# The squares of a norm's second half: four tiles added on GpSimd and summed once on TensorE

## The chip, the core and the metric

The kernel runs on one core of a Trainium2 chip. The metric is the device time of one launch in microseconds. TensorE multiplies matrices, VectorE and ScalarE do elementwise work, GpSimd does slower elementwise work on SBUF, SyncE issues most of the loads. The engines have a queue each and meet at semaphores.

## The reference

Two transformer blocks follow each other on x (1 x 512 tokens x 1024 channels, fp32). Cut to what matters here:

```python
def rms_norm(x, g):
    y = xf * lax.rsqrt(jnp.mean(xf * xf, axis=-1, keepdims=True) + NORM_EPS)
    return (y * g.astype(jnp.float32)).astype(x.dtype)

# first block, after attention and convolution
x = x + (g_a * y_attn + g_b * y_conv) @ w_out[l]
x = x + conv_ffn(rms_norm(x, norm2_g[l]), ffn_w_up[l], ...)
# second block, after its mixing
x = x + gate_m * mixed            # mixed = ... @ w_out[l]
h = rms_norm_2(x, ffn_norm_g[l]) * (1 + scale_f) + shift_f
u, v = jnp.split(h @ w_up[l], 2, axis=-1)
```

The change touches two norms: `norm2_g` of the first block and `ffn_norm_g` of the second. Each stands between the output projection (`w_out`) and the projection up (`w_up`).

## The kernel before

Activations lie turned: channels on the 128 partitions, eight tiles of channels (`KD` = 8), and the 512 tokens in the free dimension. A projection is a run of tiles s, numbered through the whole program; each makes 128 output channels. The first norm stands after tiles `S_OUT` = 50 to 57 and before `S_UP` = 58; the other after `S_OUT2` = 148 to 155 and before `S_UP2` = 156.

**Weights.** Products are split in two parts for precision. For a tile, SyncE loads the raw weights (two tiles a buffer, two buffers), ScalarE rounds them to `w_hi` (`hi`), GpSimd subtracts to get `w_lo` (`lo`, line 778), and TensorE makes three products for each of the eight tiles of its input: `split_product`, lines 2120 to 2122. `hi` waits for its buffers; `lo(s)` waits for `hi_done` and counts `lo_done`, on which both TensorE and the next load into the raw buffer wait.

**The norm in halves.** `split_norm` (VectorE), `split_norm_act` (ScalarE) and `into_split_norm`, `first_sum`, `second_sum` and `ffn_pe` (TensorE) split the tokens in two halves, `COLS[0]` and `COLS[1]`, of 256 each. Index b is 0 for the first norm and 2 for the other. The last four of the eight output tiles are computed half by half. ScalarE squares x in twelve steps q (`square_of`): q 0 to 3 are tiles 0 to 3 in full width, q 4 to 7 the first halves of tiles 4 to 7, q 8 to 11 their second halves, written to `hn` (two buffers) and `sq` (two buffers). VectorE adds the squares q 1 to 7 to `rstd` (`half_add`, semaphore `half_added`). So `rstd` holds in its first half the squares of all eight tiles, in its second half only those of tiles 0 to 3.

The sum over the partitions is a matmul with a 128x128 matrix of ones in plain fp32. `first_sum` (line 2173) makes it once over the first half of `rstd`. `second_sum` makes five into the same PSUM columns: one of `rstd` (line 2177), and one of each of the four squares q 8 to 11 (line 2180), each after a wait for its square. Then ScalarE takes the root (`half_root`, line 879), VectorE the reciprocal (line 1354) and scales the eight tiles of this half (lines 1361, 1369, 1371), ScalarE rounds them.

**The order around the second sum** is written by hand, in each engine's queue:
- TensorE (`ffn_pe`): first halves of the first two up tiles, then `second_sum`, first halves of the third and fourth, then the second halves of all four.
- ScalarE: `hi` of the four up tiles, with the squares 8 to 11 and the rounded pieces of the first half between them; the last `hi` stands just before the last square.
- GpSimd: nothing but the `lo` of the four up tiles (`lo(s)` in loops over s, in the second norm at the end of `hgrn_pool`), then a hardware loop over the rest of the up tiles.
- SyncE: the load for the seventh and eighth up tile waits for the `lo` of the fourth.

Of the kernel before, what the change touches and what calls it, by code (L numbers as in the profile page):

```python
# [10 lines left out]
ALU = mybir.AluOpType  # L11
# [7 lines left out]
KD = D // P  # L19
# [23 lines left out]
S_ATTN, S_CONV, S_OUT, S_UP, S_DOWN = 34, 42, 50, 58, 102  # L43
S_FH, S_QH, S_KV2, S_PAIRED, S_GH = 126, 130, 134, 136, 144
S_OUT2, S_UP2, S_DOWN2, S_END = 148, 156, 200, 224
# [113 lines left out]
def build(nc, a, out):  # L159
# [5 lines left out]
    with ctx:  # L165
# [29 lines left out]
        ones = sb("ones", [P, P])  # L195
        small = sb("small", [P, NSM, P])
        sm = small[:, :, :].rearrange("p a b -> p (a b)")
        rstd = sb("rstd", [P, T])
# [104 lines left out]
        ps = [nc.alloc_psum_tensor(f"ps{i}", [P, 512], F32) for i in range(8)]  # L303
# [14 lines left out]
        squared, summed, rooted, inverted = sem("squared"), sem("summed"), sem("rooted"), sem("inverted")  # L318
        normed, n_hi = sem("normed"), sem("n_hi")
        half_done, x_half, half_added, half_lo = sem("half_done"), sem("x_half"), sem("half_added"), sem("half_lo")  # L320
# [76 lines left out]
        for n in range(S_END // 2):  # L397
            s = 2 * n
# [69 lines left out]
        COLS = [slice(0, HALF), slice(HALF, T)]  # L468
        SPLIT_FROM = [S_OUT, S_FH - 4, S_OUT2]
        SQUARES, SQUARES2, PIECES = 12, KD + 2, 2 * KD  # L470

        SQ_BASE, HALF_SQ = {2: SQUARES, 5: SQUARES2 + 2 * SQUARES}, [0, SQUARES, SQUARES2 + SQUARES]
        HALF_SUM = [0, None, 2]
        HALF_HN = [0, PIECES, 2 * PIECES]
        HALF_ROOT = [QT, QT + 2, QT + 4]
        HALF_DONE, HALF_ADDED = [0, 4, 6], [0, None, KD - 1]


        SUM_COLS = [slice(64 + 4 * half, 68 + 4 * half) for half in range(2)]
# [18 lines left out]
        def square_of(q):  # L498

            k = q if q < KD else q - 4  # L500
            cols = slice(0, T) if q < 4 else COLS[q // KD]
            return k, cols, rstd[:, :] if q == 0 else (hn, sq)[k // 2 % 2][:, k % 2, cols]
# [107 lines left out]
        def hgrn_pool(pool, lo):  # L610

            def level(n):
                b = ALL[n]
                g, f, k = pairs_of(hg, b), pairs_of(hf, b), pairs_of(hk, b)
                if n:
                    kk = pairs_of(keys_at[n], b)
                    earlier = [m for m in range(1, n) if keys_at[m] is keys_at[n]]
                    if earlier:
                        pool.wait_ge(chunk_done, level_done(earlier[-1] + 1))
                    pool.tensor_tensor(kk[:, :, 0, :], k[:, :, 0, :], g[:, :, 0, :], ALU.mult).then_inc(k_scaled, 1)  # L620
                if n < len(ALL) - 1:
                    if n:
                        pool.wait_ge(f_merged, n)
                    pool.tensor_tensor(g[:, :, 0, :], g[:, :, 0, :],
                                       f[:, :, 1, b - 1:b].to_broadcast([P, HG * T // (2 * b), b]),
                                       ALU.mult).then_inc(g_merged, 1)
                    pool.wait_ge(g_merged, n + 1)

            def gated_head(hd):
                pool.wait_ge(r_sq, hd + 1)  # L630
                pool.wait_ge(freed["act"], FREED[S_GH + hd][1])
                pool.tensor_tensor(hq[:, hd, :], hq[:, hd, :], hgo[:, hd, :], ALU.mult).then_inc(r_gated, 1)

            pool.wait_ge(f_ready, 2 * HG)
            level(0)
            lo(S_KV2)
            lo(S_KV2 + 1)
            lo(S_PAIRED)
            lo(S_PAIRED + 1)
            level(1)  # L640
            for s in range(S_PAIRED + 2, S_PAIRED + 5):
                lo(s)
            level(2)
            lo(S_PAIRED + 5)
            level(3)
            level(4)
            lo(S_PAIRED + 6)
            level(5)
            lo(S_PAIRED + 7)
            level(6)  # L650
            lo(S_GH)
            level(7)
            level(8)
            lo(S_GH + 1)
            for s in range(S_GH + 2, S_OUT2 + 1):
                lo(s)
            gated_head(0)
            lo(S_OUT2 + 1)
            for hd in range(1, HG):
                gated_head(hd)  # L660
                if hd == 2:
                    lo(S_OUT2 + hd)
            for s in range(S_OUT2 + 3, S_UP2 + 4):
                lo(s)

        block = ctx.enter_context(nc.Block())

# [87 lines left out]
        @block.gpsimd  # L755
        def _(pool):
            chain = [0]

            def link(ins):
                chain[0] += 1  # L760
                ins.then_inc(pool_chain, 1)
                pool.wait_ge(pool_chain, chain[0])

            link(pool.memset(ident[:, :], 0.0))
            link(pool.affine_select(out=ident[:, :], in_=ident[:, :], compare_op=ALU.not_equal, fill=1.0,
                                    base=0, pattern=[[-1, P]], channel_multiplier=1))
            pool.memset(eps_t[:, :], EPS)
            pool.memset(ones[:, :], 1.0).then_inc(consts, 1)
            link(pool.memset(rows[:, NSM - 1, :], 0.0))
            small_dmas(pool, 1)  # L770

            def lo(s, slot=None, count=None):

                pool.wait_ge(hi_done, s + 1 if count is None else count)
                slot = s if slot is None else slot
                nk = 8 if count is not None else DEPTH_OF[s]
                part = raw[slot // 2 % 2][:, 0:nk * 256].rearrange("p (k n) -> p k n", k=nk)
                pool.tensor_tensor(w_lo[slot % 4][:, 0:nk, :], part[:, :, slot % 2 * P:(slot % 2 + 1) * P],  # L778
                                   w_hi[slot % 4][:, 0:nk, :].bitcast(F32), ALU.subtract).then_inc(lo_done, 1)

            def tables():
                link(pool.iota(dist[:, :], [[-1, T]], base=T - P, channel_multiplier=1,
                               allow_small_or_imprecise_dtypes=True))
                link(pool.affine_select(out=dist[:, :], in_=dist[:, :], compare_op=ALU.is_ge, fill=MASKED,
                                        base=T - P, pattern=[[-1, T]], channel_multiplier=1))
                cpat = [[P, QT], [-CMP_STRIDE, 32]]
                link(pool.iota(cdist[:, :, :], cpat, base=1 - CMP_BLOCK, channel_multiplier=1,
                               allow_small_or_imprecise_dtypes=True))
                link(pool.affine_select(out=cdist[:, :, :], in_=cdist[:, :, :], compare_op=ALU.is_ge, fill=MASKED,
                                        base=1 - CMP_BLOCK, pattern=cpat, channel_multiplier=1))  # L790
                link(pool.memset(cvalid[:, :, :], 1.0))
                pool.affine_select(out=cvalid[:, :, :], in_=cvalid[:, :, :], compare_op=ALU.is_ge, fill=0.0,
                                   base=1 - CMP_BLOCK, pattern=cpat, channel_multiplier=1).then_inc(consts, 1)
                pool.memset(vcN[:, :], 0.0)
                pool.memset(pcT[:, :, :], 0.0)
                pool.memset(z[:, :, 0:PAD], 0.0).then_inc(consts, 1)

            for s in range(S_UP + 4):
                lo(s)
                if s == 2:  # L800
                    tables()
            with pool.Fori(0, FT // 2 - 1) as i:
                for j in range(4):
                    lo(None, S_UP + j, i * 4 + (S_UP + j + 5))
            for s in range(S_DOWN, S_KV2):
                lo(s)
                if S_DOWN + 5 <= s < S_DOWN + 19 and (s - S_DOWN) % 2:
                    masks2(pool, link, (s - S_DOWN - 5) // 2)
                if s in (S_QH, S_QH + 1):
                    for m in range(2):  # L810
                        tables2(pool, link, 2 * (s - S_QH) + m)
            tables2(pool, link, 4)
            hgrn_pool(pool, lo)
            with pool.Fori(0, FT // 2 - 1) as i:
                for j in range(4):
                    lo(None, S_UP2 + j, i * 4 + (S_UP2 + j + 5))
            for s in range(S_DOWN2, S_END):
                lo(s)
# [1298 lines left out]
        def _(pe):  # L2117
# [56 lines left out]

            def second_sum(b):
                pe.wait_ge(normed, HALF_HN[b] + KD)
                pe.matmul(ps[7][:, COLS[1]], ones[:, :], rstd[:, COLS[1]], start=True, stop=False)
                for q in range(KD, SQUARES):
                    pe.wait_ge(squared, HALF_SQ[b] + q + 1)
                    ins = pe.matmul(ps[7][:, COLS[1]], ones[:, :], square_of(q)[2], start=False, stop=q == SQUARES - 1)  # L2180
                ins.then_inc(summed, 1)

            def into_split_norm(b, x, xl, ready, after=lambda n: None):

# [164 lines left out]
            for j in range(1, NI + 2):  # L2349
# [5 lines left out]
                if j <= NI:  # L2355
                    m = j - 1
                    i, t, b = ITEMS1[m]
# [398 lines left out]
```

## Time and profile before

| | us |
|---|---|
| median of 3 runs | 1392.86 |
| the runs | 1390.56 to 1392.98 |
| the profiled execution | 1392.87 |
| its span | 1391.0 |
| TensorE matmul busy | 1377.5 |
| GpSimd busy | 594.9 |
| VectorE busy | 775.9 |
| ScalarE busy | 598.9 |

The span is the stretch from the first to the last instruction in the trace. Busy times are sums over one engine's instructions; matmuls are pipelined, so their records overlap, and the distance between the starts of two of them tells what one costs. In the rows PE is TensorE, DVE VectorE, ACT ScalarE, POOL GpSimd and SP SyncE; names stand as out<-in. `few` in a row is the small tile of epsilons.

### The profile page before, as it was taken

Reading aid. Unit: us, or ns where it says so; the run is one execution under the profiler, and the core shown is the slowest. Engines: PE = TensorE matmul, PEld = TensorE weight load, DVE = VectorE, ACT = ScalarE, POOL = GpSimd, SP = SyncE. Lnnn points to the kernel's source line nnn. Section 1 sums busy time; section 2 is a strip of 40 time slices with the busy share of each in tenths; the row PEclk is TensorE's granted clock in tenths of the full one; section 3 lists DMA queues with packets and bytes.
Section 4 is the critical chain, followed back from the end, with each engine's and each line's share of the span. In section 5 each row is a group of like instructions: output and inputs, shape, how many; then the busy total and the mean of one; then the engine's idle time right before and its main releaser. Section 6 shows DMA issues by size and latency. Waiting matters only on the chain.

```text
span 1391.0 us, 20905 instructions
## 1 busy us (share of the span) xinstructions
PE 1377.5 (99%) x7666; PEld 1147.1 (82%) x7666; DVE 775.9 (56%) x1524; ACT 598.9 (43%) x1030; POOL 594.9 (43%) x314
## 2 busy tenths in 40 slices
PE   8999999999999999999999999999999999999998
PEld 7877777778998888888889978878898888888887
DVE  5897865456677666666884878522563323231222
ACT  7223555464255445443222525575354444342222
POOL 7432222216244444444543479523345444444441
PEclk9999999999999999999999999999999999999999
DMA  7931111015525444445662241121213233222321
GB/s 219 218 92 61 31 62 46 19 44 167 167 77 181 136 138 151 150 131 161 202 209 83 65 117 61 31 61 31 92 61 121 90 102 110 90 87 87 106 84 61
DMA packets 188309, 146.15 MB, mean 105 GB/s; under 512 B 21561, under 2 KB 186659, under 8 KB 188240
## 3 DMA queue, kind: packets, MB, share of 16 engines
q1 hardware_dynamic: 186528, 144.59, 33.9%
q8 instruction: 47, 0.77, 0.2%
q10 hardware_dynamic: 1200, 0.36, 0.1%
q0 software_dynamic: 512, 0.25, 0.1%
q14 instruction: 22, 0.18, 0.0%
HBM read 143.08 MB, written 2.10 MB: 104 GB/s over the span
## 4 chain that ended last, share of the span: by engine, by line
PE 91%; DVE 5%; DMA 2%; issue 1%; ACT 0%; DVEq 0%; ACTq 0%
PE ps L2120 27%; PE ps L2121 26%; PE ps L2122 26%; DMA ada<-in_ada_w 2%; DVE ps L1736 2%; PE ps L2564 2%; PE ps L2308 2%; PE ps L2391 1%; PE ps L2374 1%; PE ps L2621 1%; PE ps L2591 1%; PE ps L2644 1%; PE ps L2656 1%; PE ps L2206 0%; PE ps L2388 0%
## 5 line engine op out<-in xcount | busy, mean ns | idle before, releaser
L778 POOL TENSOR_TENSOR w_lo<-raw,w_hi 128x1024 fp32r<-128x1024 f32 (+2 forms) x224 | 515.5, 2305 | 726.4 <-ACT w_hi L843 448.5
L2120 PE MATMUL ps<-h_hi,w_hi 128*128 128x512 f32 (+1 forms) x1336 | 505.2, 378 | 0.6 <-DVE h_lo L1371 0.6
L2121 PE MATMUL ps<-h_lo,w_hi 128*128 128x512 f32 (+1 forms) x1336 | 494.3, 370 | 0.0
L2122 PE MATMUL ps<-h_hi,w_lo 128*128 128x512 f32 (+1 forms) x1336 | 494.2, 370 | 0.0
L2120 PEld LDWEIGHTS ps<-h_hi,w_hi 128*128 128x128 f32 x1336 | 252.3, 189 | 60.5 <-issue 17.7
L2122 PEld LDWEIGHTS ps<-h_hi,w_lo 128*128 128x128 f32 x1336 | 252.2, 189 | 43.2
L2121 PEld LDWEIGHTS ps<-h_lo,w_hi 128*128 128x128 f32 x1336 | 252.6, 189 | 39.9 <-issue 0.5
L843 ACT ACTIVATE w_hi<-raw 128x1024 fp32r<-128x1024 f32 (+2 forms) x136 | 133.6, 984 | 265.5 <-PE ps L2122 256.4
L1111 ACT ACTIVATE w_hi<-raw 128x1024 fp32r<-128x1024 f32 x88 | 93.2, 1059 | 218.0 <-PE ps L2122 218.0
L2120 PE MATMUL ps<-g_hi,w_hi 128*128 128x512 f32 (+1 forms) x394 | 146.8, 373 | 0.0
L2121 PE MATMUL ps<-g_lo,w_hi 128*128 128x512 f32 (+1 forms) x394 | 144.7, 367 | 0.0
L2122 PE MATMUL ps<-g_hi,w_lo 128*128 128x512 f32 (+1 forms) x394 | 144.6, 367 | 0.0
L1736 DVE SCALAR_TENSOR_TENSOR ps<-ada,cond,ps 128x128 f32<-128x128 f32 x288 | 102.5, 356 | 10.3
L2122 PEld LDWEIGHTS ps<-g_hi,w_lo 128*128 128x128 f32 x394 | 74.3, 189 | 12.3
L2121 PEld LDWEIGHTS ps<-g_lo,w_hi 128*128 128x128 f32 x394 | 74.4, 189 | 11.5
L2120 PEld LDWEIGHTS ps<-g_hi,w_hi 128*128 128x128 f32 x394 | 74.4, 189 | 11.5
L1775 DVE SCALAR_TENSOR_TENSOR sq<-ps,small,sq 128x511 f32<-128x511 f32 x44 | 33.0, 750 | 88.5 <-ACT sq L1118 85.4
L2045 DVE SCALAR_TENSOR_TENSOR xT<-ps,small,xT 128x256 f32<-128x256 f32 (+1 forms) x22 | 13.3, 604 | 106.2 <-PE ps L2122 106.2
L1512 DVE SCALAR_TENSOR_TENSOR ps<-z,small,ps 128x512 f32<-128x512 f32 x106 | 70.4, 755 | 0.0
L1769 DVE TENSOR_TENSOR hn<-ps,sq 128x512 f32<-128x512 f32 x22 | 15.2, 691 | 85.9 <-ACT sq L1122 85.9
L1010 ACT ACTIVATE sc<-sc,stat 128x128 f32<-128x128 f32 (+3 forms) x64 | 35.5, 555 | 38.8 <-DVE stat L1525 38.8
L1655 DVE COPY pT<-ps 128x128 f32<-128x128 f32 (+3 forms) x32 | 15.7, 490 | 52.2 <-PE ps L2374 52.2
(364 smaller groups left out, 1707.8 us busy)
## 6 DMA issues: line engine op xcount, KB each, us to landing
ada<-in_ada_w SPq DMA_DIRECT2D x48, 512.0 KB, 3.8
raw<-in_ffn_w_up SPq DMA_DIRECT2D x22, 1024.0 KB, 5.0
raw<-in_w_up SPq DMA_DIRECT2D x22, 1024.0 KB, 4.9
raw<-in_w_in SPq DMA_DIRECT2D x21, 1024.0 KB, 5.1
raw<-in_ffn_w_down SPq DMA_DIRECT2D x8, 896.0 KB, 5.7
raw<-in_w_down SPq DMA_DIRECT2D x8, 896.0 KB, 4.7
raw<-in_w_in SPq DMA_DIRECT2D x16, 256.0 KB, 3.8
raw<-in_w_out SPq DMA_DIRECT2D x4, 1024.0 KB, 5.1
```

The source lines that it names most:

```text
L778: pool.tensor_tensor(w_lo[slot % 4][:, 0:nk, :], part[:, :, slot % 2 * P:(slot % 2 + 1) * P], w_hi[slot % 4][:, 0:nk, :].bitcast(F32), ALU ...
L843: act.activation(w_hi[s % 4][:, 0:nk, :], part[:, :, s % 2 * P:(s % 2 + 1) * P], ACT.Copy).then_inc(hi_done, 1)
L1010: act.activation(x, x, ACT.Exp, scale=-1.0, bias=stat[:, 2 * (j % 2) + g:2 * (j % 2) + g + 1], accum_out=stat[:, 4 + 2 * (j % 2) + g:5 + 2 ...
L1111: act.activation(w_hi[s % 4][:, :, :], part[:, :, s % 2 * P:(s % 2 + 1) * P], ACT.Copy).then_inc(hi_done, 1)
L1512: ins = dve.scalar_tensor_tensor(out=out, in0=src, scalar=w, in1=was, op0=ALU.mult, op1=ALU.add)
L1736: dve.scalar_tensor_tensor(out=acc, in0=src, scalar=c, in1=acc, op0=ALU.mult, op1=ALU.add).then_inc(ada_scaled, 1)
L1775: dve.scalar_tensor_tensor(out=u[:, t, 1:T], in0=src[:, 0:T - 1], scalar=col(wname, m + wide), in1=u[:, t, 1:T], op0=ALU.mult, op1=ALU.add ...
L2120: pe.matmul(out_ap, w, x, start=first, stop=False, **kw)
L2121: pe.matmul(out_ap, w, xl, start=False, stop=False, **kw)
L2122: return pe.matmul(out_ap, wl, x, start=False, stop=last, **kw)
L2308: pe.matmul(ps[4 + g][:, 0:L], qT[grp, i, t * P:(t + 1) * P], kT[grp, b, 0:L], start=True, stop=True).then_inc(qk_done, 1)
L2564: ins = pe.matmul(bank[:, at:at + nq], keys[:, hd, t * P:(t + 1) * P], qd[n % 2][:, hd, q0:q0 + nq], start=True, stop=True)
```

## The change

In both norms GpSimd adds the four squares q 8 to 11 to the second half of `rstd`, in order, each add waiting for its square and for the add before. TensorE's `second_sum` waits for the last of these adds (`half_added` at `HALF_ADDED[b]` + 11) and makes one matmul instead of five. Since `half_added` now counts four more in the first norm, the base for the second (`HALF_ADDED[2]`) becomes 11.

```diff
--- before.py
+++ after.py
@@ -473,7 +473,7 @@
         HALF_SUM = [0, None, 2]
         HALF_HN = [0, PIECES, 2 * PIECES]
         HALF_ROOT = [QT, QT + 2, QT + 4]
-        HALF_DONE, HALF_ADDED = [0, 4, 6], [0, None, KD - 1]
+        HALF_DONE, HALF_ADDED = [0, 4, 6], [0, None, SQUARES - 1]
 
 
         SUM_COLS = [slice(64 + 4 * half, 68 + 4 * half) for half in range(2)]
@@ -661,7 +661,17 @@
                 if hd == 2:
                     lo(S_OUT2 + hd)
             for s in range(S_OUT2 + 3, S_UP2 + 4):
+                if s == S_UP2 + 3:
+                    add_late_squares(pool, 2)
                 lo(s)
+
+        def add_late_squares(pool, b):
+
+            for q in range(KD, SQUARES):
+                _, cols, src = square_of(q)
+                pool.wait_ge(squared, HALF_SQ[b] + q + 1)
+                pool.wait_ge(half_added, HALF_ADDED[b] + q - 1)
+                pool.tensor_tensor(rstd[:, cols], src, rstd[:, cols], ALU.add).then_inc(half_added, 1)
 
         block = ctx.enter_context(nc.Block())
 
@@ -796,6 +806,8 @@
                 pool.memset(z[:, :, 0:PAD], 0.0).then_inc(consts, 1)
 
             for s in range(S_UP + 4):
+                if s == S_UP + 3:
+                    add_late_squares(pool, 0)
                 lo(s)
                 if s == 2:
                     tables()
@@ -2174,11 +2186,8 @@
 
             def second_sum(b):
                 pe.wait_ge(normed, HALF_HN[b] + KD)
-                pe.matmul(ps[7][:, COLS[1]], ones[:, :], rstd[:, COLS[1]], start=True, stop=False)
-                for q in range(KD, SQUARES):
-                    pe.wait_ge(squared, HALF_SQ[b] + q + 1)
-                    ins = pe.matmul(ps[7][:, COLS[1]], ones[:, :], square_of(q)[2], start=False, stop=q == SQUARES - 1)
-                ins.then_inc(summed, 1)
+                pe.wait_ge(half_added, HALF_ADDED[b] + SQUARES - 1)
+                pe.matmul(ps[7][:, COLS[1]], ones[:, :], rstd[:, COLS[1]], start=True, stop=True).then_inc(summed, 1)
 
             def into_split_norm(b, x, xl, ready, after=lambda n: None):
 
```

The names in the rows below: `w_lo_55` to `w_lo_58` and `w_hi_51` to `w_hi_54` are the four slots of the split weights. TensorE in the first norm, from the end of the second up tile's first half to the start of the third's. Before:

```order
L2121 MATMUL ps<-h_lo,w_hi_54 128x256
L2122 MATMUL ps<-h_hi,w_lo_58 128x256
L2177 MATMUL ps<-rstd,ones 128x256
L2180 MATMUL ps<-hn,ones 128x256 x2
L2180 MATMUL ps<-sq,ones 128x256 x2
L2120 MATMUL ps<-h_hi,w_hi_51 128x256
L2121 MATMUL ps<-h_lo,w_hi_51 128x256
```

Now:

```order
L2133 MATMUL ps<-h_lo,w_hi_54 128x256
L2134 MATMUL ps<-h_hi,w_lo_58 128x256
L2190 MATMUL ps<-rstd,ones 128x256
L2132 MATMUL ps<-h_hi,w_hi_51 128x256
L2133 MATMUL ps<-h_lo,w_hi_51 128x256
```

Behind the matmul on `rstd` the four on `hn` and `sq` are gone; what precedes stays.

GpSimd in the first norm, the `lo` of the up tiles, which in this stretch are the four ahead of the branch into the loop. Before:

```order
L778 TENSOR_TENSOR w_lo_57<-raw_50,w_hi_53 128x1024 [waits hi_done]
L778 TENSOR_TENSOR w_lo_58<-raw_50,w_hi_54 128x1024 [waits hi_done]
L778 TENSOR_TENSOR w_lo_55<-raw_49,w_hi_51 128x1024 [waits hi_done]
L778 TENSOR_TENSOR w_lo_56<-raw_49,w_hi_52 128x1024 [waits hi_done]
L802 UNCONDITIONAL_BRANCH
L802 ISA
L778 TENSOR_TENSOR w_lo_57<-raw_50,w_hi_53 128x1024 [waits hi_done]
```

Now:

```order
L788 TENSOR_TENSOR w_lo_57<-raw_50,w_hi_53 128x1024 [waits hi_done]
L788 TENSOR_TENSOR w_lo_58<-raw_50,w_hi_54 128x1024 [waits hi_done]
L788 TENSOR_TENSOR w_lo_55<-raw_49,w_hi_51 128x1024 [waits hi_done]
L674 TENSOR_TENSOR rstd<-hn,rstd 128x256 [waits half_added,squared] x2
L674 TENSOR_TENSOR rstd<-sq,rstd 128x256 [waits half_added,squared] x2
L788 TENSOR_TENSOR w_lo_56<-raw_49,w_hi_52 128x1024 [waits hi_done]
L814 UNCONDITIONAL_BRANCH
L814 ISA
L788 TENSOR_TENSOR w_lo_57<-raw_50,w_hi_53 128x1024 [waits hi_done]
```

The four adds stand ahead of the fourth up tile's `lo`; the second norm has the same, `lo` with the same slots. ScalarE's, VectorE's and SyncE's queues hold the same instructions in the same order.

## Rows read from the trace of the kernel before

**Rows 1.** The page's table of engines: busy us, share of the span, instructions.

```profile
PE 1377.5 (99%) x7666; PEld 1147.1 (82%) x7666; DVE 775.9 (56%) x1524; ACT 598.9 (43%) x1030; POOL 594.9 (43%) x314
```

**Rows 2.** TensorE by stretches, first norm: stretch, length, busy (records), clock, DMA share, GB/s.

```profile
396.40:399.00 2.60, 2.60 (x16) 1.00 0.79 208
```

**Rows 3.** Timeline of TensorE at the second sum, first norm: start, duration, engine, operation.

```profile
396.35 0.28 PE L2122 MATMUL ps<-h_hi,w_lo 128*128 128x256 f32 x1
396.47 0.60 PE L2177 MATMUL ps<-rstd,ones 128*128 128x256 f32 x2
396.91 1.03 PE L2180 MATMUL ps<-hn,ones 128*128 128x256 f32 x4
397.77 1.03 PE L2180 MATMUL ps<-sq,ones 128*128 128x256 f32 x4
...
398.75 0.28 PE L2121 MATMUL ps<-h_lo,w_hi 128*128 128x256 f32 x1
```

**Rows 4.** Timeline of TensorE at the first norm's first sum.

```profile
381.53 0.28 PE L2122 MATMUL ps<-h_hi,w_lo 128*128 128x256 f32 x1
381.65 0.60 PE L2173 MATMUL ps<-rstd,ones 128*128 128x256 f32 x2
...
382.20 0.28 PE L2121 MATMUL ps<-h_lo,w_hi 128*128 128x256 f32 x1
```

**Rows 5.** Timeline of TensorE at the other norm's second sum.

```profile
1023.52 0.28 PE L2122 MATMUL ps<-h_hi,w_lo 128*128 128x256 f32 x1
1023.64 0.60 PE L2177 MATMUL ps<-rstd,ones 128*128 128x256 f32 x2
...
1025.92 0.28 PE L2121 MATMUL ps<-h_lo,w_hi 128*128 128x256 f32 x1
```

**Rows 6.** Timeline of GpSimd in both norms.

```profile
389.80 2.41 POOL L778 TENSOR_TENSOR w_lo<-raw,w_hi 128x1024 fp32r<-128x1024 f32 x1 [0.50 <-ACT w_hi L843]
392.81 2.40 POOL L778 TENSOR_TENSOR w_lo<-raw,w_hi 128x1024 fp32r<-128x1024 f32 x1 [0.60 <-ACT w_hi L843]
...
1017.34 2.40 POOL L778 TENSOR_TENSOR w_lo<-raw,w_hi 128x1024 fp32r<-128x1024 f32 x1 [0.84 <-ACT w_hi L843]
1020.74 2.41 POOL L778 TENSOR_TENSOR w_lo<-raw,w_hi 128x1024 fp32r<-128x1024 f32 x1 [1.00 <-ACT w_hi L843]
```

**Rows 7.** Timeline of ScalarE in both norms: late squares, root of the first norm.

```profile
390.82 0.42 ACT L875 ACTIVATE sq<-xT 128x256 f32<-128x256 f32 x1 [0.82 <-DVE xT L1750]
...
392.66 0.42 ACT L875 ACTIVATE sq<-xT 128x256 f32<-128x256 f32 x1
...
398.83 0.45 ACT L879 ACTIVATE ps<-ps,few 128x256 f32<-128x256 f32 x1 [5.75 <-PE ps L2180]
...
1020.68 0.42 ACT L875 ACTIVATE sq<-xT 128x256 f32<-128x256 f32 x1
```

**Rows 8.** Timeline of GpSimd and of VectorE elsewhere, GpSimd subtracting 512 columns.

```profile
320.83 1.74 POOL L778 TENSOR_TENSOR w_lo<-raw,w_hi 128x512 fp32r<-128x512 f32 x1 [0.98 <-ACT w_hi L843]
323.55 1.29 POOL L778 TENSOR_TENSOR w_lo<-raw,w_hi 128x512 fp32r<-128x512 f32 x1 [0.98 <-ACT w_hi L843]
...
320.74 0.68 DVE L1699 TENSOR_TENSOR cv_lo<-acc,cv_hi 128x512 fp32r<-128x512 f32 x1
```

**Rows 9.** Timeline of GpSimd, a chain linked by its own semaphore.

```profile
673.66 0.36 POOL L580 TENSOR_SCALAR_AFFINE_SELECT msk_f<-msk_f 128x64 f32<-128x64 f32 x1
674.09 0.34 POOL L582 TENSOR_SCALAR_AFFINE_SELECT msk_f<-msk_f 128x64 f32<-128x64 f32 x1
```

**Rows 10.** Timeline of VectorE beside the fourth w_lo of the first norm.

```profile
392.93 2.31 DVE L1736 SCALAR_TENSOR_TENSOR ps<-ada,cond,ps 128x128 f32<-128x128 f32 x6
```

**Rows 11.** Timeline of SyncE, DMA issues from 390 to 415 us, timeline of ScalarE.

```profile
396.08 0.57 SPq L678 DMA_DIRECT2D raw<-in_ffn_w_up  x1
...
raw<-in_ffn_w_up SPq DMA_DIRECT2D x1, 1024.0 KB, 7.1
...
413.22 1.06 ACT L1111 ACTIVATE w_hi<-raw 128x1024 fp32r<-128x1024 f32 x1
```

## The prediction

> **What bounds the kernel now.** I read the page's engine table first. TensorE's matmul rows are busy for 1377.5 of 1391.0 us and GpSimd's for 594.9 [rows 1], so time falls only where TensorE itself gets less to do or waits less. Then TensorE by stretches: around the second sum of the first norm it is busy throughout, with the granted clock at 1.00, the upper of its two levels (2.4 GHz) [rows 2]. The list of waits names nothing at all for TensorE between 380 and 420 us or between 1005 and 1050 us, the two places that are changed. So what its queue no longer holds there should come off the end, unless the new wait takes it back. That makes two questions: what TensorE spends on the four matmuls that go, and whether GpSimd has the sum ready by the time TensorE comes to it.
>
> Both sides are against the profiled execution: 1392.87 us, span 1391.0 plus 1.9 around it. The median of the runs is 1392.86, so nothing has to be carried over; the runs lie between 1390.56 and 1392.98.
>
> **Removed from TensorE: 1.73 us per norm.** Each 128x256 matmul against the ones matrix in plain fp32 is two records. Their durations overlap, so I go by distances between starts. The products around them start every 0.12 us. Take the last L2122 before a sum and the first L2121 behind it: undisturbed they are 0.24 us apart.
> - First half's sum, one matmul: 381.53 to 382.20 is 0.67, less 0.24 = 0.43 us [rows 4].
> - Second half's sum, five matmuls: 396.35 to 398.75 is 2.40, less 0.24 = 2.16 us [rows 3], which is 5 x 0.43.
> - In the other norm 1023.52 to 1025.92 is again 2.40, so 2.16 us [rows 5].
>
> With the change the second half's sum is one matmul like the first half's. It should cost 0.43, so each norm saves 2.16 - 0.43 = 1.73 us and both 3.46 us. Order and work of the other TensorE instructions stay.
>
> **Added on GpSimd: four adds of 128x256 per norm, from the end of the third w_lo on.** The queue puts them behind the w_lo of the third tile and ahead of that of the fourth. The trace has no add of this size there. Nearest are subtractions with the same two SBUF operands: 2.40 us for 1024 columns [rows 6] and 1.29 for 512 [rows 8]. That is 1.11/512 = 2.17 ns a column, and for 256 columns 1.29 - 0.555 = 0.735 us. A quarter of the 1024-column one, 0.60, is the lower bound; the whole 512-column one, 1.29, the upper. I take 0.735, since the line through both sizes leaves little fixed cost. Each add waits for the one before by semaphore; the linked chain of GpSimd shows 0.07 us for that (673.66 + 0.36 = 674.02, next start 674.09) [rows 9]. So 0.805 us an add and 3.22 for four.
>
> The Trainium skill (GPSIMD Engine Reference, "When to use GPSIMD") speaks against such a move: an elementwise operation with two inputs belongs on VectorE, being about twice as fast there. Its measured 4497 ns for 2048 columns (same page, "Performance versus the Vector engine") would make an add here an estimated 0.56 us plus start-up; taken as the price it would leave the sum at 3.46, as the add would still be hidden.
>
> **Does it hide?** First norm: the third w_lo ends at 389.80 + 2.41 = 392.21 [rows 6]. Three of the four squares are written by 391.24 (390.82 + 0.42); the last ends at 392.66 + 0.42 = 393.08 [rows 7], before the fourth add wants it (392.21 + 3 x 0.805 = 394.6). So GpSimd's own pace decides: done at 395.43. TensorE's sum starts at 396.47 [rows 3]: 1.04 us to spare. Second norm: 1017.34 + 2.40 = 1019.74 [rows 6], last square 1021.10 [rows 7], fourth add from 1022.2, done at 1022.96. TensorE is there at 1023.64 [rows 5]: 0.68 us to spare. The new wait costs nothing. In the tighter norm it stays so up to 3.90/4 = 0.975 us an add.
>
> **What is queued behind the adds.** The fourth tile's w_lo, 2.41 us: it now ends at 395.43 + 2.41 = 397.84 instead of 395.21, and at 1025.37 instead of 1023.15. TensorE needs it for the first half of the fourth tile, after the sum (0.43) and 24 products of the third (2.88): 396.35 + 0.12 + 0.43 + 2.88 = 399.78, and 1026.95. To spare: 1.9 and 1.6 us. Nothing. Behind that w_lo waits SyncE's load of the raw buffer: it was issued at 396.08 and landed 7.1 us later; now some 1.8 us later, about 405. ScalarE's first read of it was at 413.22, now 411.5 [rows 11]. Nothing; the second norm has the same order.
>
> **What hangs on the sum** (root, reciprocal, 16 half-pieces, then TensorE's second halves) starts when the sum ends, and TensorE's third tile starts then too. Both move earlier by the same 1.73 us, so no gap opens between them; every later transfer and copy is released by one of the two. ScalarE has idled for 5.75 us when the root starts at 398.83 [rows 7], so it can take the root sooner. Nothing is added for this.
>
> **A rule that could price the adds otherwise.** Twice in the trace a 512-column subtraction on GpSimd took 1.74 instead of 1.29 us, and beside it VectorE ran a TENSOR_TENSOR with both inputs in SBUF [rows 8]. Beside the multiply-adds of VectorE with one input in SBUF and one in PSUM, w_lo kept its 2.40 us [rows 6, 10]. That is what the Trainium skill says (GPSIMD Engine Reference, "Specifications"): GpSimd shares SBUF interfaces with VectorE and collides with its instructions in a 2-port mode or with two SBUF inputs; the trace agrees. During the adds VectorE runs only operations that take at least one operand from PSUM or read one tile, as beside w_lo today. By row and by rule alike the 0.735 stands; if the 1.74 row held here, the third rival would follow.
>
> **Sum:** 1392.87 - 3.46 = **1389.4 us**, 0.25% faster. About 0.2% (2.8 us) is what a measurement of this kernel can tell from no change. The forecast lies only 0.7 us beyond that.
>
> **Rivals.**
> - *The adds are late by a little.* An add costs its upper bound, 1.29 + 0.07 = 1.36 us. Four take 5.44: done at 397.65 and 1025.18, and TensorE stands still for 1.18 and 1.54 us. Left of the gain: 3.46 - 2.72 = 0.74, so 1392.1. For it: no add of this size is in the trace, and spans on GpSimd are rough. Against it: the two sizes that are there give a price near the proportional one.
> - *The saving is not passed on.* Something of fixed pace behind the norms (a load, the reciprocal chain, the code at the start of the feed-forward loop) holds TensorE, which arrives earlier and waits: 1392.9. Against it: no wait of TensorE at either place, and the load has over 6 us. For it: I haven't followed every queue through the loops.
> - *GpSimd's queue becomes the bound, and the kernel is slower.* The place is TensorE's wait ahead of the sum. With a period p per add TensorE stands still for 4p - 4.26 in the first norm and 4p - 3.90 in the second. Gain and loss balance where 8p - 8.16 = 3.46, p = 1.45 us; it is slower by over 0.2% from p = 1.80. At the collided size, 1.74 + 0.07 = 1.81, done at 399.45 and 1026.98: 2.98 + 3.34 - 3.46 = 2.86 us slower, 1395.7. For it: adds read two SBUF tiles, and such a collision cost 0.45 us once. Against it: even the 512-column operation took that only beside a VectorE instruction of another kind.
>
> **How the numbers follow.** The forecast gets 0.82, the late adds 0.06, the saving not passed on 0.09, the slower one 0.03. Within the forecast the scatter of the runs matters (one of three was 2.3 us below the others), and the margin over 0.2% is only 0.7 us: I give it 0.70 for faster and 0.12 for within. With both small rivals that is 0.27 within 0.2%, and 0.03 slower. The range begins 1.4 us under the forecast (some of the scatter, and no mechanism gives more) and ends at the late adds' 1392.1.
>
> **What the profile after would show.** Right: at 396.47 and 1023.64 one L2190 sum of two records, the next L2121-type product 0.55 us behind it instead of 2.28; no wait of TensorE on GpSimd; adds near 0.74 us at distances of 0.81, the first from 392.2; the fourth w_lo ending near 397.8; the root at about 397.1; a span of about 1387.5. Wrong: a TensorE wait on GpSimd's add (first rival, or third if over 1.7 us), new TensorE waits behind the norms that sum to about 3 us (second rival), or a saving per norm other than 1.73 us.

## The result and the profile after

| | before | after |
|---|---|---|
| median, us | 1391.90 (10 runs) | 1388.92 (10 runs) |
| runs, us | 1390.56 to 1394.81 | 1387.22 to 1389.63 |
| profiled execution, us | 1392.87 | 1389.02 |
| its span, us | 1391.0 | 1387.0 |
| TensorE matmul busy | 1377.5 | 1374.0 |

The ratio after to before is 0.9971 with a 95% interval of 0.9963 to 0.9978: 0.29% faster, clear of the 0.2% that can be told. The ratio is worked out over all runs and is not the quotient of the medians, which differ by 2.98 us or 0.21%. The page of after, its head and engine table, against [rows 1]:

```profile
span 1387.0 us, 20891 instructions
...
PE 1374.0 (99%) x7650; PEld 1143.2 (82%) x7650; DVE 773.9 (56%) x1524; ACT 599.2 (43%) x1030; POOL 601.6 (43%) x322
```

TensorE at the second sums of the two norms, against [rows 3, 5] (timeline: start, duration, engine, line, operation):

```profile
397.61 0.28 PE L2134 MATMUL ps<-h_hi,w_lo 128*128 128x256 f32 x1
397.73 0.60 PE L2190 MATMUL ps<-rstd,ones 128*128 128x256 f32 x2
397.97 0.47 PE L2132 MATMUL ps<-h_hi,w_hi 128*128 128x256 f32 x1
398.28 0.28 PE L2133 MATMUL ps<-h_lo,w_hi 128*128 128x256 f32 x1
...
1021.23 0.28 PE L2134 MATMUL ps<-h_hi,w_lo 128*128 128x256 f32 x1
1021.35 0.60 PE L2190 MATMUL ps<-rstd,ones 128*128 128x256 f32 x2
1021.59 0.47 PE L2132 MATMUL ps<-h_hi,w_hi 128*128 128x256 f32 x1
1021.90 0.28 PE L2133 MATMUL ps<-h_lo,w_hi 128*128 128x256 f32 x1
```

From the last L2134 to the first L2133 behind the sum it is 398.28 - 397.61 = 0.67 us and 1021.90 - 1021.23 = 0.67; the same pair was 2.40 apart before. The saving is 1.73 us in each norm. In front of the sum no gap stands.

GpSimd in both norms, against [rows 6]:

```profile
391.06 2.41 POOL L788 TENSOR_TENSOR w_lo<-raw,w_hi 128x1024 fp32r<-128x1024 f32 x1 [0.49 <-ACT w_hi L855]
393.43 1.63 POOL L674 TENSOR_TENSOR rstd<-hn,rstd 128x256 f32<-128x256 f32 x2
395.20 1.63 POOL L674 TENSOR_TENSOR rstd<-sq,rstd 128x256 f32<-128x256 f32 x2
396.78 2.38 POOL L788 TENSOR_TENSOR w_lo<-raw,w_hi 128x1024 fp32r<-128x1024 f32 x1
...
1015.04 2.40 POOL L788 TENSOR_TENSOR w_lo<-raw,w_hi 128x1024 fp32r<-128x1024 f32 x1 [0.83 <-ACT w_hi L855]
1017.39 1.64 POOL L674 TENSOR_TENSOR rstd<-hn,rstd 128x256 f32<-128x256 f32 x2
1019.18 1.62 POOL L674 TENSOR_TENSOR rstd<-sq,rstd 128x256 f32<-128x256 f32 x2
1020.76 2.38 POOL L788 TENSOR_TENSOR w_lo<-raw,w_hi 128x1024 fp32r<-128x1024 f32 x1
```

From the end of the third w_lo to the end of the last add it is 396.83 - 393.47 = 3.36 us in both norms, 0.84 an add. The pairs show what that is made of: they start 1.77 us apart, so an add follows the one before after 0.88 us, and a pair lasts 1.63, so an add takes 1.63 - 0.88 = 0.75 us and the link between two 0.14. The adds end 0.90 us ahead of TensorE's sum in the first norm (395.20 + 1.63 = 396.83 against 397.73), 0.55 in the other (1020.80 against 1021.35). ScalarE, against [rows 7, 11]: the last square, the root, and the first rounding that needs the delayed load. SyncE: that load.

```profile
393.92 0.42 ACT L887 ACTIVATE sq<-xT 128x256 f32<-128x256 f32 x1
398.36 0.45 ACT L891 ACTIVATE ps<-ps,few 128x256 f32<-128x256 f32 x1 [4.02 <-PE ps L2190]
...
412.75 1.06 ACT L1123 ACTIVATE w_hi<-raw 128x1024 fp32r<-128x1024 f32 x1
```

```profile
399.19 0.37 SPq L688 DMA_DIRECT2D raw<-in_ffn_w_up  x1
```

Up to the sum everything lies 1.26 us later than in the trace of before (397.73 against 396.47), so the root at 398.36 stands for 397.10 and the end of the fourth w_lo at 399.16 for 397.90. The delayed load is issued at 399.19 and is read at 412.75 without a wait.

**Where the rest of the 4.0 us between the two traces is.** ScalarE's roundings w_hi follow each other alike in both, so their starts tell how much later (+) or earlier (-) after is at each place:

| at | before | after | after less before, us | since the row above |
|---|---|---|---|---|
| ahead of the attention | 129.52 | 129.22 | -0.30 | -0.30 |
| 10 us on | 139.07 | 140.35 | +1.28 | +1.58 |
| ahead of the first norm | 382.66 | 383.92 | +1.26 | -0.02 |
| behind it | 409.98 | 409.51 | -0.47 | -1.73 |
| late in the recurrence | 948.98 | 948.24 | -0.74 | -0.27 |
| 17 us on | 965.79 | 963.50 | -2.29 | -1.55 |
| behind the other norm | 1037.22 | 1033.19 | -4.03 | -1.74 |

Two entries have nothing to do with the change: TensorE's granted clock fell once in each of the two executions, in another place. TensorE by stretches (start:end, length, busy and records, clock, DMA share, GB/s), before and then after:

```profile
130.00:140.00 10.00, 9.54 (x63) 1.00 0.34 106
960.00:970.00 10.00, 10.00 (x51) 0.83 0.00 0
```

```profile
130.00:140.00 10.00, 9.54 (x54) 0.83 0.34 106
960.00:970.00 10.00, 10.00 (x55) 1.00 0.00 0
```

A mean of 0.83 over 10 us is a loss of 1.7 us of full speed. The two falls nearly cancel (+1.58 and -1.55), 3.47 of the 4.03 us stand at the two norms, and the remaining 0.59 (the rows -0.30, -0.02 and -0.27) stand at places that the change doesn't touch and were not traced to a cause.

### The profile page after: what moved, and what is told of

Its sections match the earlier page's. It is cut to its first block, busy times and chain, and to the rows that moved or that the text cites. A ratio compares the mean times of both kernels' runs of the same rounds, so it can differ in the third digit from the quotient of the medians.

```text
span 1387.0 us, 20891 instructions
## 1 busy us (share of the span) xinstructions
PE 1374.0 (99%) x7650; PEld 1143.2 (82%) x7650; DVE 773.9 (56%) x1524; ACT 599.2 (43%) x1030; POOL 601.6 (43%) x322
## 4 chain that ended last, share of the span: by engine, by line
PE 91%; DVE 5%; DMA 3%; issue 1%; ACT 0%; DVEq 0%; SPq 0%; ACTq 0%
PE ps L2132 27%; PE ps L2134 26%; PE ps L2133 26%; DMA ada<-in_ada_w 2%; DVE ps L1748 2%; PE ps L2573 2%; PE ps L2317 2%; PE ps L2400 1%; PE ps L2383 1%; PE ps L2630 1%; PE ps L2600 1%; PE ps L2653 1%; PE ps L2665 1%; DMA x_in<-in_x 0%; PE ps L2397 0%
## 5 line engine op out<-in xcount | busy, mean ns | idle before, releaser
L2133 PE MATMUL ps<-h_lo,w_hi 128*128 128x512 f32 (+1 forms) x1336 | 494.0, 370 | 0.0
L2134 PE MATMUL ps<-h_hi,w_lo 128*128 128x512 f32 (+1 forms) x1336 | 493.7, 370 | 0.0
L2134 PEld LDWEIGHTS ps<-h_hi,w_lo 128*128 128x128 f32 x1336 | 252.2, 189 | 43.3
L2133 PEld LDWEIGHTS ps<-h_lo,w_hi 128*128 128x128 f32 x1336 | 252.4, 189 | 40.2 <-issue 0.5
L2133 PE MATMUL ps<-g_lo,w_hi 128*128 128x512 f32 (+1 forms) x394 | 144.6, 367 | 0.0
L2134 PE MATMUL ps<-g_hi,w_lo 128*128 128x512 f32 (+1 forms) x394 | 144.4, 367 | 0.0
L2134 PEld LDWEIGHTS ps<-g_hi,w_lo 128*128 128x128 f32 x394 | 74.3, 189 | 12.2
L2133 PEld LDWEIGHTS ps<-g_lo,w_hi 128*128 128x128 f32 x394 | 74.4, 189 | 11.5
```

The costliest lines, as they stand in the source:

```text
L2133: pe.matmul(out_ap, w, xl, start=False, stop=False, **kw)
L2134: return pe.matmul(out_ap, wl, x, start=False, stop=last, **kw)
```

## The experiments

All runs were timed in five rounds beside the kernel before, in three calls with a chip each; each ratio is against before in its own call. "Over the change" is against 1388.9, the change's median from the first timing, and so goes across calls.

| run | median, us | ratio to before, 95% interval |
|---|---|---|
| the change | 1388.92 | 0.9971 (0.9963 to 0.9978) |
| the change once more | 1387.97 | 0.9970 (0.9957 to 0.9982) |
| first norm alone | 1391.12 | 0.9991 (0.9982 to 1.0000) |
| no adds | 1389.52 | 0.9978 (0.9969 to 0.9987) |
| adds and all matmuls | 1391.76 | 0.9996 (0.9987 to 1.0006) |
| adds on VectorE | 1392.07 | 0.9994 (0.9985 to 1.0003) |
| the same, w_lo held back | 1389.04 | 0.9976 (0.9965 to 0.9986) |
| six adds | 1393.53 | 1.0005 (0.9996 to 1.0014) |
| eight adds | 1397.12 | 1.0037 (1.0026 to 1.0049) |
| adds behind w_lo | 1395.19 | 1.0023 (1.0014 to 1.0032) |
| rounded sums | 1387.95 | 0.9967 (0.9957 to 0.9977) |
| rounded sums and chunks | 1385.23 | 0.9949 (0.9936 to 0.9963) |

**The first norm alone.**

```diff
-                if s == S_UP2 + 3:
-                    add_late_squares(pool, 2)
+                if b == 2:
+                    pe.matmul(ps[7][:, COLS[1]], ones[:, :], rstd[:, COLS[1]], start=True, stop=False)
+                    for q in range(KD, SQUARES):
...
```

> The change in the first norm alone; the other norm keeps its five matmuls and no adds. Theory (TensorE is saved 1.73 us per norm, adds free): half the gain, 1.7 us, so about 1390.2 by the median of before (1391.9); in the trace the first norm's sum costs 0.43 us by distances of starts, the other's 2.16. Rival (the gain is not in the sums but in something the change shifted, such as the clock): the gain is whole or gone.

The median, 1391.12, is 0.9 us above the expected 1390.2; by the ratio it is 0.0009 x 1392 = 1.3 us, interval 0 to 2.5. So the timing agrees with 1.7 us and can't quite tell it from nothing. The trace decides: the first norm's sum takes two records and the other's ten, the first norm keeps step with the trace of after, and across the other norm it falls behind it by 1.72 us, by roundings at the same places.

**No adds, one matmul.**

```diff
-                if s == S_UP + 3:
-                    add_late_squares(pool, 0)
...
-                pe.wait_ge(half_added, HALF_ADDED[b] + SQUARES - 1)
+                pe.wait_ge(squared, HALF_SQ[b] + SQUARES)
```

> TensorE makes one matmul per second sum and nobody adds the late squares: the squares of tiles 4 to 7 of the second half are left out of the norm. Theory (the adds are hidden): the same time as the change, 1388.9, within 0.7 us; TensorE's matmul after the sum starts at the same distance, 0.55 us. Rival (the adds or the delayed w_lo cost something): faster than the change by more than 1 us.

1389.52, no faster than the change; the intervals overlap, and the product behind the sum starts 0.55 us after it, as in the trace of after. Four adds and a fourth w_lo that comes later cost nothing that can be measured.

**Adds and all five matmuls.**

```diff
                 pe.wait_ge(half_added, HALF_ADDED[b] + SQUARES - 1)
-                pe.matmul(ps[7][:, COLS[1]], ones[:, :], rstd[:, COLS[1]], start=True, stop=True).then_inc(summed, 1)
+                pe.matmul(ps[7][:, COLS[1]], ones[:, :], rstd[:, COLS[1]], start=True, stop=False)
+                for q in range(KD, SQUARES):
...
```

> GpSimd adds the late squares and TensorE still makes all five matmuls after them, so the late squares count twice in the norm. Theory: the time of before, 1391.9, within 0.7 us, since the adds and their wait are hidden and the matmuls cost what they did. Rival (the adds cost TensorE time): slower than before by over 1 us.

1391.76 against 1391.80 for before in the same call. Adds alone change nothing, and it is the four matmuls that carry the gain: over both norms this trace loses 1.70 and 1.73 us to that of after.

**The adds on VectorE.** The same sums, made where an add is quicker.

```diff
-                if s == S_UP + 3:
-                    add_late_squares(pool, 0)
...
                 second_half(7)
+                for q in range(KD, SQUARES):
+                    half_add(b, q)
                 between_halves()
```

> The same sums, but VectorE makes the four late adds, between its last residual and the ada reduction, instead of GpSimd. Theory: only TensorE's four matmuls count, so the same time as the change, 1388.9, within 0.7 us. In the first norm the ada reduction ends some 2.2 us later, near 397.8 on the clock of before, and may hold the reciprocal by 0.2 us, which TensorE does not see. Rival (VectorE, being quicker at an add, is the better place, as the rule of the notes on GpSimd says): faster than the change by over 1 us.

Missed: 1392.07, 3.2 us over the change and no better than before. VectorE's timeline in both norms, then GpSimd's at the same time:

```profile
392.76 2.96 DVE L1358 TENSOR_TENSOR rstd<-hn,rstd 128x256 f32<-128x256 f32 x2
395.82 0.95 DVE L1358 TENSOR_TENSOR rstd<-sq,rstd 128x256 f32<-128x256 f32 x2
...
399.69 1.76 DVE L1362 RECIPROCAL ps<-ps 128x256 f32<-128x256 f32 x1
...
1020.44 2.96 DVE L1358 TENSOR_TENSOR rstd<-hn,rstd 128x256 f32<-128x256 f32 x2
1023.50 0.96 DVE L1358 TENSOR_TENSOR rstd<-sq,rstd 128x256 f32<-128x256 f32 x2
```

```profile
393.02 2.42 POOL L786 TENSOR_TENSOR w_lo<-raw,w_hi 128x1024 fp32r<-128x1024 f32 x1 [0.59 <-ACT w_hi L851]
...
1020.60 2.50 POOL L786 TENSOR_TENSOR w_lo<-raw,w_hi 128x1024 fp32r<-128x1024 f32 x1 [0.99 <-ACT w_hi L851]
```

Two adds that need 0.95 us take 2.96, and both times they are through only when GpSimd's w_lo is (393.02 + 2.42 = 395.44; 1020.60 + 2.50 = 1023.10). By the single records of the trace the first add of the pair takes its usual 0.42 us; the second, begun 0.26 and 0.35 us after w_lo, takes 2.44. In the first norm the ada reduction (the multiply-adds of [rows 10]) behind them pushes the reciprocal to 399.69, 1.6 us after the root's end, and TensorE gets its h_lo late: waits of 0.5 us are listed, and from 404 to 406 us it starts 10 records where it starts 19 in the next 2 us. In the other TensorE waits for the sum:

```profile
PE ps L2188 <- DVE rstd L1358: 0.9, 1, 0.9
```

By roundings at the same places it loses 1.59 us to after in the first norm and 1.17 in the other, 2.76 together, so 0.7 of the 3.46 are left; the ratio says 0.8, with an interval that reaches 0. The mechanism is the one that [rows 8] showed from the other side, and the Trainium skill names it (GPSIMD Engine Reference, "Specifications": GpSimd's SBUF interfaces are shared with VectorE, with contention for its instructions that have two SBUF inputs). In [rows 8] GpSimd began 0.09 us after VectorE and lost 0.45 us; here VectorE's second add began after GpSimd and lost 2.0, nearly a whole w_lo. Both times the one that began later lost.

**The same with w_lo held back.** If the collision is the cause, keeping GpSimd still must bring the gain back. Against the run before:

```diff
+                if s == S_UP + 3:
+                    pool.wait_ge(half_added, HALF_ADDED[0] + SQUARES - 1)
                 lo(s)
...
```

> As the kernel with the late adds on VectorE, but GpSimd holds its fourth w_lo back until VectorE's last add. Theory (VectorE's adds with two SBUF inputs stood still while GpSimd's w_lo ran): the four adds take 0.42 us each again, the last ends 2.3 us after the first begins instead of 4.0, TensorE's second sum waits for nothing, and the time comes back to within 0.7 us of the change: 1388.9 to 1389.6. Rival (the adds themselves, or the ada reduction pushed back behind them, cost the 3 us): it stays near 1392.

It does: 1389.04. VectorE, then GpSimd, first norm:

```profile
392.60 0.95 DVE L1362 TENSOR_TENSOR rstd<-hn,rstd 128x256 f32<-128x256 f32 x2
393.65 0.95 DVE L1362 TENSOR_TENSOR rstd<-sq,rstd 128x256 f32<-128x256 f32 x2
```

```profile
394.69 2.40 POOL L788 TENSOR_TENSOR w_lo<-raw,w_hi 128x1024 fp32r<-128x1024 f32 x1 [2.43 <-DVE rstd L1362]
```

The adds are at 0.95 us a pair again and done at 394.60, and the held w_lo, which starts 1.8 us later, costs nothing that shows. Which engine adds makes no difference here, as long as the two don't work on SBUF pairs at once.

**Eight adds.** How much room is there, and what does a late sum cost? `EXTRA` is 4 here and 2 in the run with six.

```diff
+            for n in range(EXTRA):
+                pool.wait_ge(half_added, HALF_ADDED[b] + SQUARES - 1 + n)
+                pool.tensor_tensor(rstd[:, cols], src, rstd[:, cols], ALU.add).then_inc(half_added, 1)
...
```

> GpSimd makes eight adds per norm instead of four, the last four of the same square again, so that square counts five times; TensorE waits for the eighth. Theory (an add takes 0.84 us by distances of starts, and TensorE comes 0.90 us after the fourth add in the first norm, 0.55 in the other): TensorE waits 3.36 - 0.90 = 2.5 and 3.36 - 0.55 = 2.8 us on GpSimd, so 5.3 us over the change: 1394.2. Rival (there is more room, since what hangs on the sum is not what TensorE needs first): less than 3 us over the change.

8.2 us over the change, not 5.3. The waits are 2.27 and 2.61 us, 0.2 less than expected:

```profile
PE ps L2194 <- POOL rstd L678: 4.9, 2, 2.6
```

```profile
395.82 3.13 POOL L678 TENSOR_TENSOR rstd<-sq,rstd 128x256 f32<-128x256 f32 x4
```

The extra adds, which wait for one semaphore each, follow each other after 0.80 us, where the four of the change, which wait for two, do so after 0.88.

The rest lies behind them. TensorE's timeline in the first norm, then by stretches:

```profile
399.10 0.67 PE L2194 MATMUL ps<-rstd,ones 128*128 128x256 f32 x2 [2.27 <-POOL rstd L678]
...
400.79 0.41 PE L2136 MATMUL ps<-h_hi,w_hi 128*128 128x256 f32 x1
401.00 0.41 PE L2137 MATMUL ps<-h_lo,w_hi 128*128 128x256 f32 x1
401.21 0.41 PE L2138 MATMUL ps<-h_hi,w_lo 128*128 128x256 f32 x1
```

```profile
396.80:399.10 2.30, 0.03 (x1) 1.00 0.80 228
399.10:400.50 1.40, 1.40 (x10) 1.00 0.00 0
400.50:403.60 3.10, 3.10 (x17) 0.51 0.35 103
403.60:407.00 3.40, 3.40 (x29) 0.95 0.62 215
```

1.4 us after the wait the products start every 0.21 us and not every 0.12: the clock fell to its lower level, 0.51 on average over 3.1 us, and came back. By roundings at the same places the trace loses 3.99 us in the first norm and 4.22 in the other, 1.6 to 1.7 us more than each wait.

That is the profiled execution (1398.17 us). Its mean granted clock over the whole run is 0.996; the profiled executions with one fall in all have 0.998 or 0.999, as have all 16 timed runs of the change. Of the nine timed runs here two have 0.998 and took 1394.7 and 1395.5 us, near the expected 1394.2; the two at 0.996 took 1397.1 and 1398.2, the three at 0.994 and 0.995 took 1399.2 to 1401.2. So the waits cost what was expected, and what comes on top is the clock, which falls in most executions and not in all.

**The adds behind the fourth w_lo.** The calls moved one step down the queue.

```diff
-                if s == S_UP + 3:
-                    add_late_squares(pool, 0)
                 lo(s)
...
+            add_late_squares(pool, 0)
...
```

> The four adds stand behind the w_lo of the fourth up tile instead of ahead of it. Theory: they end 3.35 us after that w_lo, at 398.6 and 1026.5 on the clock of before, where TensorE comes to its sum at 396.5 and 1023.6: waits of 2.1 and 2.9 us, 5.0 us over the change, 1393.9. Rival (the place in GpSimd's queue does not matter): 1388.9.

6.3 us over the change, so slower than before by 0.23%. In its profile the waits are 2.03 and 2.78 us, with the same fall of the clock behind both (0.50 over 3.2 us):

```profile
PE ps L2188 <- POOL rstd L673: 4.8, 2, 2.8
```

The profiled execution (1397.47 us, mean clock 0.996) is the second slowest of eleven. Six of the eleven have a mean clock of 0.998 and took 1394.3 to 1395.2 us, 0.4 to 1.3 over the expected 1393.9: with a mean like that of executions that have one fall in all, they can hardly have had one behind both waits. The place in GpSimd's queue is worth more than the change itself, with or without the clock.

**Six adds.**

> Six adds per norm on GpSimd, the last two of the same square again, so that square counts three times. Theory: TensorE waits 1.68 - 0.90 = 0.8 us in the first norm and 1.68 - 0.55 = 1.1 us in the other. If waits that short leave TensorE's granted clock at 1.00, the time is 1.9 us over the change, 1390.8. Rival (the clock falls to half behind these waits too, as it did behind waits of 2.0 us and more in the runs with eight adds and with the adds behind w_lo, at about 1.6 us each): 5.1 us over the change, 1394.

```profile
PE ps L2194 <- POOL rstd L678: 1.7, 2, 1.0
```

```profile
130.00:140.00 10.00, 9.54 (x58) 0.83 0.35 106
398.80:403.00 4.20, 4.13 (x33) 1.00 0.54 140
960.00:970.00 10.00, 10.00 (x57) 0.83 0.00 0
1026.00:1031.00 5.00, 4.99 (x40) 1.00 0.28 78
```

TensorE waits 0.67 and 1.02 us, and in this trace its clock stays at 1.00 behind both (398.8 and 1026.0). The trace loses 0.89 and 1.26 us in the two norms, as the theory has it. Yet the median is 4.6 us over the change (4.9 by the two ratios of this call), near the rival's number.

The profile has two falls of the clock, at 130 and at 960 us, where that of after has one, at 130. Its 4.7 us over the trace of after are 0.9 and 1.3 at the norms, 1.6 at the second fall, and 1.0 elsewhere, ahead of 110 us and around 825. The timed runs point the same way: eight of the eleven have a mean clock of 0.997, as the profiled one, and took 1393.2 to 1394.0 us; the other three have 0.998 and took 1391.6 to 1391.9. Those three lie 0.8 to 1.1 us over the expected 1390.8. So the median is high because most executions lost about one fall more than the change does. Whether the additional falls come from the waits is open: in the one execution that is profiled both stand elsewhere, and the first of them ahead of the norms.

**The change once more**, unaltered.

> The change itself once more, unaltered, to see what repeats: 1388.9 within 0.7 us. In its trace the two sums cost 0.43 us each again; the stretch of half clock that stood at 132 to 136 us may stand elsewhere or be missing, and moves everything behind it by 1.5 us.

The ratio is 0.9970 (0.9957 to 0.9982), as before; the median of six, 1387.97, is 0.9 us lower and so just outside the 0.7 expected. The two sums cost 0.43 us each again. The profiled execution (1390.43) has its fall at 960 us and not at 130, and lies 1.5 us behind the trace of after from its first 11 us on: the clock is not the only source of scatter.

**Rounded sums.** The gain per matmul taken comes from its plain fp32 form, so the four that are left were tried in the rounded type of the products.

```diff
-        ones = sb("ones", [P, P])
+        ones = sb("ones", [P, P], F32R)
...
+                dst = h_hi[:, KD - 1, COLS[1]] if q == SQUARES - 1 else rstd[:, cols]
...
-                pe.matmul(ps[7][:, COLS[1]], ones[:, :], rstd[:, COLS[1]], start=True, stop=True).then_inc(summed, 1)
+                pe.matmul(ps[7][:, COLS[1]], ones[:, :], h_hi[:, KD - 1, COLS[1]], start=True, stop=True).then_inc(summed, 1)
...
```

> The change, and the last add of each half writes its result rounded into a column tile of h_hi that is free, so that all four sums by ones are matmuls of the rounded type and not of plain fp32; ones is written by GpSimd as 0 * ident + 1. Theory (a sum costs 0.43 us since plain fp32 takes two records of 0.2 us and slow starts around them): each costs about 0.12 like the products, 4 x 0.31 = 1.2 us less than the change, 1387.7. Rival (the switch between kinds costs as much): 1388.9.

```profile
395.68 0.28 PE L2136 MATMUL ps<-h_hi,w_lo 128*128 128x256 f32 x1
395.80 0.28 PE L2192 MATMUL ps<-h_hi,ones 128*128 128x256 f32 x1
395.92 0.28 PE L2134 MATMUL ps<-h_hi,w_hi 128*128 128x256 f32 x1
```

The sum is one record and costs 0.12 us, like a product. 1387.95: the trace gains 1.2 us on that of after across the four sums, as expected, but the timing can't tell them from the change (0.9957 to 0.9977 against 0.9963 to 0.9978).

**Rounded sums and chunks.** The same for the six 512-column sums of the recurrence: VectorE writes their products rounded, through a second name for hn. Against the run before:

```diff
+        hn_r = sb("hn_r", [P, 2, T], F32R, at=offset[0] - 2 * T * 4)
...
-                out = hn[:, c % 2, :]
+                out = hn_r[:, c % 2, :]
...
```

> The kernel with the rounded sums, and VectorE also writes the products that TensorE sums by ones for the first six chunks of the recurrence rounded (128x512 each), so those six matmuls are of the rounded type too. Theory: a 512-column sum in plain fp32 takes two records at 0.43 us distance, the rounded one 0.23: 6 x 0.63 = 3.8 us less than the kernel with rounded sums, 1384.1, if TensorE is the bound there too. Rival (TensorE waits there for VectorE's products): no more than 1 us less.

TensorE's groups for these sums, before and now:

```profile
L2550 PE MATMUL ps<-hn,ones 128*128 128x512 f32 x12 | 5.6, 592 | 0.0
```

```profile
L2562 PE MATMUL ps<-hn_r,ones 128*128 128x512 f32 x6 | 1.8, 389 | 0.0
```

12 records became 6. 1385.23, 0.51% under before and the fastest kernel of the study. Between 794 and 873 us, around the six sums, its trace gains 3.53 us on that of after (3.8 expected), where the kernel with rounded sums keeps step. By the medians it is 2.7 us under that kernel, with five runs, 1383.87 to 1387.66. Both rounded kernels carry their sums with less precision than the change.

## Why the forecast came out as it did

Forecast 1389.4, measured 1388.92. That the two are only 0.5 us apart is partly luck: the base was 0.97 us too high, and the medians differ by 2.98 and not by 3.46. The steps in their order:

- **TensorE is the bound, no wait at either place: right.** No-adds and adds-and-all-matmuls separate the two sides, and only the matmuls count.
- **1.73 us per norm, 3.46 in all: right.** Read as 2.40 - 0.67 in both norms. The measured ratio, with its interval, is 3.1 to 5.2 us of 1392; 3.46 lies in it.
- **An add of 0.735 us and 0.805 with its link: the add right, the link too small.** An add took 0.75. The link was 0.14 and not 0.07: it was read from a chain with one semaphore [rows 9], and each of these adds waits for two, its square and the add before. With one semaphore, as the extra adds of the run with eight have it, an add comes every 0.80 us. From the end of w_lo it makes 0.84 an add; the room was 0.90 and 0.55 us and not 1.04 and 0.68. Nothing hung on it.
- **The fourth w_lo and the load behind it: right.** No wait of TensorE on w_lo, none of ScalarE on the load. The fourth w_lo ended at 397.90 on the clock of before (397.84 said), the load was issued 1.85 us later than before (1.8 said), and the root stood at 397.10.
- **The base: this step failed.** The prediction said that nothing had to be carried over, since the profiled execution (1392.87) and the median (1392.86) agree. That median was of three runs. Of ten it is 1391.90, and of the 33, 27 and 16 in the later calls 1391.8, 1392.2 and 1391.85. So the forecast stood 2.5 us, 0.18%, under before as it is, less than the 0.2% that it claimed to pass and less than its own sum, and the measured change was 0.29%. The agreement with the profiled execution was no check, since one execution of a kernel whose runs lie 4 us apart can agree with a median of three by chance; nor does its fall of the clock at 960 us (1.5 us) explain the gap, for 10 of the 13 profiled executions have one such fall, that of after too, which lies at its own median. The three runs themselves could have warned: one was 2.3 us below the others, which the prediction saw and used for its chances only. What should have been forecast is the difference, 3.46 us, with the base's own uncertainty of about 1 us beside it.
- **The rule that elementwise work belongs on VectorE (the Trainium skill, GPSIMD Engine Reference, "When to use GPSIMD").** It was set aside because the adds are hidden. The runs say more: on VectorE the same adds are faster alone (0.95 us a pair against 1.63 on GpSimd), and in the order tried first they cost 2.8 us, by collision with w_lo. With the collision taken away both engines give the same time.
- **The slower rival: its place was right, its price too low.** It was priced by the wait alone. In the profiled executions with eight adds and with the adds behind w_lo TensorE's clock was at its lower level for about 3 us behind each of the four waits of 2.03 to 2.78 us, about 1.6 us more each; by their mean clocks the timed runs had that often, not always. The point from which that rival is over 0.2% slower lies earlier than the 1.80 us per add of the prediction: eight adds take 6.54 us from the end of w_lo, as four of 1.64 would, and were 0.37% slower than before. Gain and loss balance earlier than at its 1.45 too: six adds end 3.36 + 0.90 + 0.67 = 4.93 us behind w_lo, as four of 1.23 would, and no gain was left in the timing (1.0005), though the waits in its trace take 2.15 of the 3.46 us.

## What to carry to other kernels

A matmul that only sums may cost more than a product of the same size because of its type: read the distance between starts ahead of it and behind it, then take it off the bound engine or change its type. Before moving work to an idle engine, compute when it is done against when the bound engine comes for it, and place it by that in its queue; one step later here turned 0.29% faster into 0.23% slower. And check what the engines beside it read at that moment: VectorE and GpSimd, both with two operands from SBUF, did not run side by side. Last, the median of three runs of a kernel that scatters by 4 us is no base for a forecast of 3.5.

## What was not expected of the hardware

- VectorE's add with two SBUF inputs, begun just after a GpSimd subtraction, stood still for nearly all of it: 2.44 us for an add that takes 0.42.
- Behind four waits of 2.03 to 2.78 us TensorE's clock was at the lower level for about 3 us, in the two traces that have them, beginning at once or up to 1.4 us after the work had begun again; behind waits of 0.67 and 1.02 us it was not, in the one trace that has them. The mean clocks of the timed runs say that it does not fall there every time.
- An add on GpSimd that waits for two semaphores starts 0.14 us after the one before, with one semaphore 0.07 or 0.08.
- The scatter between executions of one kernel has a visible part: a fall of the clock (0.83 over 10 us) at 130 or near 960 us, one in 10 of the 13 profiled executions, both in two. The profiled execution of the kernel with w_lo held back has it at neither place and took 1387.77, the lowest of its runs:

```profile
130.00:140.00 10.00, 9.54 (x65) 1.00 0.34 106
960.00:970.00 10.00, 10.00 (x56) 1.00 0.00 0
```
